# High and low halves for the first attention's projections, and a lead on unnormed halves for the last gated stage

## The chip, the cores and the metric

The kernel runs on one core of one Trainium2 chip, in one launch. The metric is the device time of that core in microseconds (us); lower is better. A core has five engines that run their own instruction streams side by side and meet at semaphores: TensorE (PE, the matrix products), VectorE (DVE), ScalarE (ACT), GpSimd (POOL) and SyncE (SP, which here issues the loads of the weights). Three runs of the kernel before gave 1784.17, 1782.44 and 3429.42 us, with a median of 1784.17 us.

## The reference

The program is a small network on 256 tokens of 1024 numbers. A first block has two layers: sliding window attention with 16 query heads, 4 key and value heads and a learned sink per head, then a feed forward stage (`ffn0`); and a gated delta rule mixer with its feed forward stage (`ffn1`). A second block has `ffn2`, a convolution mixer, `ffn3`, `ffn4`, a pooling and attention mixer (`pm_in`, `pm_out`) and `ffn5`. Ahead of each stage its input is normed. In the second block the norm's gain and shift come from a condition vector, and the stage's output is gated. The two places that matter here:

```python
u = rms_norm(h, mixer_norm[0])
qkv = u @ w_in                      # q 1024, k 256, v 256 columns
q = partial_rope(rms_norm(q, q_gain), cos, sin)
k = partial_rope(rms_norm(k, k_gain), cos, sin)
...                                 # scores in a window, softmax with a sink, values
h = h + out.reshape(B, S, 1024) @ w_out

x = x + mod[:, 1, 2][:, None, :] * y          # y from the pooling and attention mixer
h = modulate(rms_norm_2(x, ffn_norm[1, 1]), mod[:, 2, 0], mod[:, 2, 1])
x = x + 0.5 * mod[:, 2, 2][:, None, :] * swiglu(h, ...)      # ffn5
```

All data are float32.

## The kernel before

**Layout.** The stream of activations `h` lies as 8 chunks of 128 features by 256 tokens. Every weight matrix is cut into units of 128 x 1024 numbers (512 KB). SP loads the units in one fixed order into a ring of five slots (`weight_ring`). A slot is free again when the unit's products are done (`unit_done`), or, for a unit that is split into halves, when its low half is written (`lo_ready`).

**Two kinds of product.** A plain product (L1074, L1259, L2355) multiplies float32 weights out of the ring by float32 activations; the trace shows it as two weight loads and two matmul records. A split product has the weights and the activations each as a high half, rounded to the type `float32r`, and a low half, the rest, and adds three products of that type: high by high, high by low, low by high (`split_product_whole`, L657 to L659). For a unit of weights ACT writes the high half (`split_hi`, L611) and DVE the low half (`split_lo`, L618) into slots of `w_hi` and `w_lo`. A slot can be written when the unit that used it before is done.

**First attention.** `attn_in` has 12 units: 10 tiles of keys and queries and 2 of values. `attn_pe` goes through turns t = 0 to 10. A turn has the product of tile t (L1074), a sum of squares over the heads of tile t-1 (L1055) and the rotation of tile t-2 (L1062); the scores of a group of four heads follow behind turns 5, 7 and 10. ACT (`attn_act`) copies and squares tile t (L1111, L1112) and takes root t-1 (L1121, L1123). DVE (`attn_dve`) norms tile t (L1149) and rotates tile t-1 (L1156 to L1159); from turn 4 on it also masks scores (L1306), takes maxima (L1316 to L1327) or divides the probabilities (L1334 to L1342). Each engine does its list in the written order. Behind the tiles come, for each of four groups b, transposes of the probabilities (L1212), the values (L1228 to L1230), a copy of the result into `mix` (`mix_copy_act`, L1291) and the output product (`out_product_pe`, L1259), two units and eight chunks n. The last group hands its chunks to `residual_dve`, where DVE adds them to `h` (L540), with the squares for the next norm beside it (L334 on ACT, L418 on DVE).

**The norm.** `norm_pe` sums the squares with a product by ones (L406), ACT takes logarithm and exponential (L357, L359), and DVE and ACT write the normed halves (`norm_dve`, L447 and L473 or L475; `norm_halves_act`, L379 or L381). PE runs a few products with no use (`warm_pe`, L395) meanwhile.

**Stages with a lead.** Where a norm's number k is in `RAW` (3, 4, 6, 7, 8), the stage's first four units (`SPLIT`) don't wait for the norm: ACT and DVE write halves of h times gain (`lead_hi_act` L282, `lead_lo_dve` L293), `lead_pe` multiplies those (L315 to L317), and the result is scaled by the root afterwards (`lead_scale_dve`, L847 and L849). Norm 9, ahead of `ffn5`, is not in `RAW`: there, three units wait for the normed halves chunk by chunk (`ffn_up_pe`, L650, L653). Ahead of it is the output product of the last mixer, `pm_out`, whose units and values are split already (L1252 to L1254, `mix_low_dve` L1300). In `ffn_dve` and `ffn_act` a unit's split stands at a fixed place of the list: units 4 and 5 of a gated stage around the sum of the first pair.

Of the kernel before, what the change touches and what calls it, by code (L numbers as in the profile page):

```python
# [15 lines left out]
F32 = mybir.dt.float32  # L16
# [8 lines left out]
T = 256  # L25
# [93 lines left out]
def build(nc, dram, out_dram):  # L119
    with ExitStack() as ctx:  # L120
# [140 lines left out]
        RAW = (3, 4, 6, 7, 8)  # L261
        GAIN_WITH_ROOT = (0, 1, 9) + RAW
        AFTER = {3: 1, 4: 2, 6: 3, 7: 4, 8: "pm_in"}
# [40 lines left out]
        def lead_pe(pe, k):  # L304
# [4 lines left out]
            for j in range(SPLIT):  # L309
                s = split_wait(pe, AFTER[k], j)  # L310
                pe.wait_ge(h_ready, C * (k - 1) + lead_bank_read(k, j))
                for c in range(C):
                    if j == 0:
                        pe.wait_ge(lead_lo_ready, leads_until(k, c))
                    nc.tensor.matmul(ps[:, j, 0:n], w_hi[:, s, c], lead[:, c, 0, 0:n], start=c == 0, stop=False, skip_group_check=True)  # L315
                    nc.tensor.matmul(ps[:, j, 0:n], w_hi[:, s, c], lead[:, c, 1, 0:n], start=False, stop=False, skip_group_check=True)
                    last = nc.tensor.matmul(ps[:, j, 0:n], w_lo[:, s, c], lead[:, c, 0, 0:n], start=False, stop=c == C - 1, skip_group_check=True)  # L317
                    if j == 0 and c == SUM_BEHIND[k]:
# [100 lines left out]

        def norm_gain_dve(dve, k):  # L420
# [18 lines left out]
        def norm_dve(dve, k):  # L439
# [4 lines left out]
            for c in range(C):  # L444
# [16 lines left out]
                if k in (3, 6) and c == 2:  # L461
                    split_lo(dve, AFTER[k], SPLIT - 1)
# [17 lines left out]
        HALVES_OF = {1: 0, 2: 1, 3: 2, 4: 3, 6: 4, 7: 5, 8: 6, 9: 7}  # L480

        def u_count(k, c):
            return U_BASE[k] + c + 1

# [83 lines left out]
        SPLIT_RUNS = [(("ffn0",), SPLIT), (("gdn_gates", "gdn_in", "gdn_out"), GDN_SPLIT), (("ffn1", "ffn2"), SPLIT), (("ffn3", "ffn4", "pm_in", "pm_out", "ffn5"), SPLIT)]  # L568
# [4 lines left out]
        for names, slots in SPLIT_RUNS:  # L573
            units = [FIRST_UNIT[name] + j for name in names for j in range(dict(UNITS)[name])]
# [50 lines left out]
        def norm_split_act(act, k, q):  # L625
# [363 lines left out]
        ax = Carver(gdn_tiles, GX)  # L989
        sco = [[ax.cut(4, 384) for _ in range(4)]]  # L990
# [7 lines left out]
        sco.append([at_.cut(4, 384) for _ in range(2)])  # L998
        assert at_.at == end

        stats = [[at_.cut(4, 3)] + [at_.cut(4, 2) for _ in range(7)] for _ in range(4)]
        alibi = at_.cut(8, 384)
# [101 lines left out]

        def attn_act(act):
            for t in range(11):
# [24 lines left out]
            mix_copy_act(act, 0, 0)  # L1131
            turned_copy_act(act, 0, 1)
# [108 lines left out]
        def out_product_pe(pe, which, b, n):  # L1241

            k = (0, 8)[which]
            first = FIRST_UNIT[LIN[k]] + 2 * b
# [3 lines left out]
            for kk in range(2 if which == 1 else 0):  # L1248
                s = split_wait(pe, "pm_out", 2 * b + kk) if n == 0 else PM_OUT_SLOTS[2 * b + kk]
                hi, lo = w_slot(s)  # L1250
# [4 lines left out]
                if n == C - 1:  # L1255
                    last.then_inc(unit_done, 1)
            for kk in range(2 if which == 0 else 0):
                s = take_unit(pe, first, kk) if n == 0 else (first + kk) % RING
                last = nc.tensor.matmul(ps[:, bank, at:at + T], ring[:, s, n], mix[:, 2 * b + kk], start=(b == 0 and kk == 0 and n < 4),  # L1259
                                        stop=(b == 3 and kk == 1), skip_group_check=True)  # L1260
# [26 lines left out]
        def mix_copy_act(act, which, b):  # L1287
            act.wait_ge(pv_ready, 4 * which + b + 1)
            oc = head_of(which, b, 0)[4]
            if which == 0:  # L1290
                nc.scalar.activation(mix[:, oc:oc + 2].rearrange("p a b -> p (a b)"), ps[:, 4, :], ACT.Copy).then_inc(mix_ready, 1)  # L1291
            else:
                nc.scalar.activation(mix_halves[:, oc:oc + 2].rearrange("p a b -> p (a b)"), ps[:, 4, :], ACT.Copy).then_inc(mix_hi_ready, 1)

        def mix_low_dve(dve, b):

            oc = head_of(1, b, 0)[4]
            flat = lambda x: x.rearrange("p a b -> p (a b)")
            dve.wait_ge(mix_hi_ready, b + 2)
# [1276 lines left out]
        def moba_pe(pe):  # L2576
# [40 lines left out]
            norm_pe(pe, 9)  # L2617
# [62 lines left out]
        def moba_dve(dve, steps):  # L2680
# [41 lines left out]
            dve.wait_ge(mix_hi_ready, 1)  # L2722
# [10 lines left out]
            mix_low_dve(dve, 0)  # L2733
# [3 lines left out]
            mix_low_dve(dve, 1)  # L2737
# [31 lines left out]
        def act_program(act):  # L2769
# [32 lines left out]
            split_hi(act, 5, SPLIT - 1)  # L2802
            ffn_act(act, 5)

        def dve_program(dve):
# [4 lines left out]
            norm_first_dve(dve)  # L2810
            angles_dve(dve, steps)
# [270 lines left out]
```

## Time and profile before

| what | value |
|---|---|
| median of three runs | 1784.17 us |
| the profiled execution | 1785.92 us, span 1784.1 us |
| TensorE busy | 1743.2 us (98%) |
| VectorE busy | 1402.2 us (79%) |
| ScalarE busy | 1028.9 us (58%) |
| GpSimd busy | 85.3 us (5%) |
| granted TensorE clock, mean | 0.998 |
| moved by DMA | 374.07 MB |

The span runs from the first to the last instruction of one profiled execution; that execution's own time is 1.8 us longer. Busy is the time in which an engine had an instruction in it. Matmuls overlap in the engine, so a long busy time doesn't mean that the engine is at its peak, and the distance between two starts says more than the length of a record. A granted clock of 1.00 is 2.4 GHz, one of 0.50 is 1.2 GHz.

### The profile page before, as it was taken

The numbers are of one execution on the slowest core, as the hardware profiler recorded it, in microseconds if no ns is written. First come the engines' busy times: TensorE is split into PE (matmuls) and PEld (weight loads), VectorE is DVE, ScalarE is ACT, GpSimd is POOL, SyncE is SP. The second block draws the span as 40 slices with busy tenths as digits, with TensorE's granted clock in tenths as the row PEclk, the third lists the DMA queues.
The fourth block names the chain that finished last, engine by engine and source line by source line (L and its number), as shares of the span: only waits on it lengthen the run. The fifth ranks groups of instructions, "written<-read, shape, count | busy, mean of one in ns | idle before, by whom it ended". The sixth has DMA issues, their size and how long they took to land.

```text
span 1784.1 us, 34769 instructions
## 1 busy us (share of the span) xinstructions
PE 1743.2 (98%) x14142; PEld 1557.7 (87%) x14142; DVE 1402.2 (79%) x2369; ACT 1028.9 (58%) x1744; POOL 85.3 (5%) x163
## 2 busy tenths in 40 slices
PE   7999999989999999999999999999999999999998
PEld 6888888888888898889988888888898889988887
DVE  4758879777766488889988977898989898867664
ACT  3657765657866477654655422665556555566553
POOL 0000001000000000001001100000101010000000
PEclk9999999999999999999999999999999999999999
DMA  5255559343332355568788933788878887436552
GB/s 196 91 186 200 190 190 347 133 144 131 102 116 96 106 199 205 189 232 308 281 294 286 337 132 112 270 307 282 321 254 311 281 318 268 161 131 205 189 189 95
DMA packets 102829, 374.07 MB, mean 210 GB/s; under 512 B 11440, under 2 KB 11600, under 8 KB 102544
## 3 DMA queue, kind: packets, MB, share of 16 engines
q1 hardware_dynamic: 80352, 289.77, 46.3%
q0 software_dynamic: 22320, 82.09, 13.4%
q8 instruction: 112, 1.84, 0.4%
q14 instruction: 45, 0.37, 0.1%
HBM read 370.74 MB, written 1.08 MB: 208 GB/s over the span
## 4 chain that ended last, share of the span: by engine, by line
PE 86%; DVE 6%; ACT 3%; issue 2%; DMA 1%; DVEq 0%; SPq 0%; ACTq 0%
PE ps L650 37%; PE ps L653 20%; PE ps L657 3%; PE ps L658 3%; PE ps L659 3%; PE ps L1074 2%; PE ps L748 2%; DVE weights_lo L618 2%; PE ps L1259 1%; PE ps L2355 1%; ACT weights_hi L611 1%; DVE arena L2474 1%; PE ps L2381 1%; DMA ffn_tiles<-in_ada 1%; PE ps L1440 1%
## 5 line engine op out<-in xcount | busy, mean ns | idle before, releaser
L618 DVE TENSOR_TENSOR weights_lo<-weight_ring,weights_hi 128x1024 fp32r<-128x1024 f32 x493 | 601.7, 1222 | 136.1 <-ACT weights_hi L611 135.4
L611 ACT ACTIVATE weights_hi<-weight_ring 128x1024 fp32r<-128x1024 f32 x493 | 518.0, 1057 | 161.9 <-PE ps L650 106.5
L650 PE MATMUL ps<-u_halves,weights_hi 128*128 128x512 f32 x2048 | 495.0, 391 | 0.9 <-DVE u_halves L473 0.5
L650 PEld LDWEIGHTS ps<-u_halves,weights_hi 128*128 128x128 f32 x2048 | 376.3, 188 | 75.8 <-DVE weights_lo L618 1.0
L653 PEld LDWEIGHTS ps<-u_halves,weights_lo 128*128 128x128 f32 x2048 | 266.0, 191 | 10.5 <-DVE weights_lo L618 0.3
L653 PE MATMUL ps<-u_halves,weights_lo 128*128 128x256 f32 x2048 | 274.2, 283 | 0.2
L650 PE MATMUL ps<-act_halves,weights_hi 128*128 128x512 f32 x952 | 231.6, 391 | 1.0 <-DVE weights_lo L618 1.0
L650 PEld LDWEIGHTS ps<-act_halves,weights_hi 128*128 128x128 f32 x952 | 173.4, 188 | 33.8 <-DVE weights_lo L618 1.4
L887 DVE SCALAR_TENSOR_TENSOR ffn_tiles<-ffn_tiles,cond 128x1024 f32<-128x1024 f32 x144 | 175.3, 1219 | 4.8 <-DMA ffn_tiles<-in_ada 4.6
L780 ACT ACTIVATE ffn_tiles<-ps 128x512 f32<-128x512 f32 x128 | 76.0, 594 | 144.1 <-PE ps L653 143.8
L653 PEld LDWEIGHTS ps<-act_halves,weights_lo 128*128 128x128 f32 x1088 | 142.3, 191 | 6.4
L653 PE MATMUL ps<-act_halves,weights_lo 128*128 128x256 f32 x1088 | 145.8, 282 | 0.0
L657 PE MATMUL ps<-u_halves,weights_hi 128*128 128x256 f32 x456 | 136.8, 300 | 4.7 <-DVE u L2062 2.9
L858 DVE TENSOR_TENSOR ffn_tiles<-ps,ffn_tiles 128x512 f32<-128x512 f32 x128 | 88.3, 689 | 59.3 <-ACT ffn_tiles L780 59.2
L983 POOL DMA_DIRECT2D ffn_tiles<-in_ada x144 | 76.1, 529 | 1215.8 <-DVE ffn_tiles L887 785.9
L658 PE MATMUL ps<-u_halves,weights_hi 128*128 128x256 f32 x456 | 129.5, 284 | 0.0
L659 PE MATMUL ps<-u_halves,weights_lo 128*128 128x256 f32 x456 | 129.3, 284 | 0.0
L334 ACT ACTIVATE u<-h 128x256 f32<-128x256 f32 x88 | 35.8, 414 | 118.4 <-DVE h L913 74.9
L657 PEld LDWEIGHTS ps<-u_halves,weights_hi 128*128 128x128 f32 x456 | 87.6, 192 | 9.2 <-DVE u L2062 3.3
L658 PEld LDWEIGHTS ps<-u_halves,weights_hi 128*128 128x128 f32 x456 | 87.9, 193 | 1.1 <-issue 1.0
L659 PEld LDWEIGHTS ps<-u_halves,weights_lo 128*128 128x128 f32 x456 | 87.8, 193 | 0.0
L793 ACT ACTIVATE ffn_tiles<-ffn_tiles 128x256 f32<-128x256 f32 x130 | 53.6, 413 | 35.5 <-DVE ffn_tiles L858 17.1
(350 smaller groups left out, 2374.6 us busy)
## 6 DMA issues: line engine op xcount, KB each, us to landing
weight_ring<-in_w SPq DMA_DIRECT2D x545, 512.0 KB, 4.0
ffn_tiles<-in_ada POOLq DMA_DIRECT2D x144, 512.0 KB, 5.8
scaled<-gates_scratch POOLq DMA_DIRECT2D x8, 512.0 KB, 5.5
arena<-in_alibi POOLq DMA_DIRECT2D x1, 1536.0 KB, 6.6
h<-in_x SPq DMA_DIRECT2D x4, 256.0 KB, 3.8
out<-u SPq DMA_DIRECT2D x4, 256.0 KB, 2.4
consts<-in_consts SPq DMA_DIRECT2D x1, 592.0 KB, 10.0
cond<-in_cond SPq DMA_DIRECT2D x1, 512.0 KB, 10.7
```

What stands on the lines that cost most here:

```text
L611: nc.scalar.activation(w_slot(s)[0], ring[:, n % RING], ACT.Copy).then_inc(hi_ready, 1)
L618: nc.vector.tensor_tensor(lo, ring[:, n % RING], hi.bitcast(F32), ALU.subtract).then_inc(lo_ready, 1)
L650: return nc.tensor.matmul(ps[:, bank], hi, halves, start=start, stop=stop, skip_group_check=True)
L653: return nc.tensor.matmul(ps[:, bank, 0:T], lo, halves[:, 0], start=start, stop=stop, skip_group_check=True)
L657: nc.tensor.matmul(out, hi, halves[:, 0], start=start, stop=False)
L658: nc.tensor.matmul(out, hi, halves[:, 1], start=False, stop=False)
L659: return nc.tensor.matmul(out, lo, halves[:, 0], start=False, stop=stop)
L780: nc.scalar.activation(corr[:, f % 2], ps[:, b:b + 2, T:2 * T], ACT.Copy).then_inc(corr_ready, 1)
L793: nc.scalar.activation(sgb[:, f % 2], src, ACT.Silu, bias=bias).then_inc(sg_ready, 1)
L858: nc.vector.tensor_tensor(gu[:, f % 3], ps[:, b:b + 2, 0:T], corr[:, f % 2], ALU.add).then_inc(gu_ready, 1)
L887: nc.vector.scalar_tensor_tensor(ada_ring[:, r], ada_ring[:, r], 1.0, cond[:], ALU.mult, ALU.mult, accum_out=mods[:, n:n + 1]).then_inc(ad ...
L983: pool.dma_start(ada_ring[:, n % 3], dram["ada"][n]).then_inc(ada_loaded[n % 3], 16)
```

## The change

Seven of the ten key and query tiles (t = 3 to 9) and the eight output units of the first attention become split products. For that `first_halves_act` and `first_halves_dve` write halves of the normed input (8 operations each), `split_hi` and `split_lo` get 15 units more, one at the end of each of the turns 0 to 9 and five behind them, and `mix_low_dve` writes the low half of each group's values on DVE. The score tiles of group 0 move from the room of `w_hi` to another place of the arena, since `w_hi` is in use now. Norm 9 joins `RAW`. `lin_residual_dve` replaces `residual_dve` ahead of it: behind each residual stands the low half of the chunk before, then seven additions of squares in pairs, where the sum on PE had three terms before. The sum stands behind chunk 3 of the lead's second unit. ACT writes the high halves of `ffn5`'s units 2 and 3 behind the last chunk. The `warm_pe` products of norm 9 are gone with its `norm_pe` at the end of `moba_pe`.

```diff
+PLAIN_QK = 3
+COUNT = dict(UNITS, attn_q=10 - PLAIN_QK)
-        RAW = (3, 4, 6, 7, 8)
-        GAIN_WITH_ROOT = (0, 1, 9) + RAW
+        RAW = (3, 4, 6, 7, 8, 9)
+        GAIN_WITH_ROOT = (0, 1) + RAW
-        SUM_BEHIND = {3: 5, 4: 4, 6: 4, 7: 4, 8: 4}
+        SUM_BEHIND = {1: (1, 7), 3: (0, 5), 4: (0, 4), 6: (0, 4), 7: (0, 4), 8: (0, 4), 9: (1, 3)}
+        def add_pairs_dve(dve, k):
+            for n, (to, other, after) in enumerate(((1, 0, 0), (3, 2, 0), (5, 4, 0), (3, 1, 2), (7, 6, 0), (5, 3, 4), (7, 5, 6))):
+                if after:
+                    dve.wait_ge(sq_added, adds_until(k, after))
+                else:
+                    dve.wait_ge(sq_ready, 8 * k + to + 1)
+                nc.vector.tensor_tensor(u[:, to], u[:, to], u[:, other], ALU.add).then_inc(sq_added, 1)
+        def lin_residual_dve(dve, k, gated, next_ffn):
...
+            for c in range(C):
...
+                nc.vector.scalar_tensor_tensor(h[:, c], ps[:, bank, at:at + T], g, h[:, c], ALU.mult, ALU.add).then_inc(h_ready, 1)
+                if c:
+                    lead_lo_dve(dve, k + 1, c - 1)
+            lead_lo_dve(dve, k + 1, C - 1)
...
+            add_pairs_dve(dve, k + 1)
+            split_lo(dve, next_ffn, 2)
-        SPLIT_RUNS = [(("ffn0",), SPLIT), ...
+        SPLIT_RUNS = [(("attn_q", "attn_out", "ffn0"), SPLIT), ...
                 if k == 9:
-                    if c == 1:
+                    if c == C - 1:
                         split_hi(act, q, 2)
+                        split_hi(act, q, SPLIT - 1)
@@ attn_pe
+                if PLAIN_QK <= t < 10:
+                    s = split_wait(pe, "attn_q", t - PLAIN_QK)
+                    for k in range(C):
+                        if t == PLAIN_QK:
+                            pe.wait_ge(u_lo_ready, 8 * HALVES_OF[0] + k + 1)
+                        last = split_product_whole(ps[:, 4 + t % 2, 0:T], w_hi[:, s, k], w_lo[:, s, k], u_halves[:, k], k == 0, k == C - 1)
+                    last.then_inc(unit_done, 1)
+        def first_halves_act(act):
+            for c in range(C):
+                act.wait_ge(u_ready, u_count(0, c))
+                nc.scalar.activation(u_halves[:, c, 0], u[:, c], ACT.Copy).then_inc(u_hi_ready, 1)
+        def first_halves_dve(dve):
+            for c in range(C):
+                dve.wait_ge(u_hi_ready, 8 * HALVES_OF[0] + c + 1)
+                nc.vector.tensor_tensor(u_halves[:, c, 1], u[:, c], u_halves[:, c, 0].bitcast(F32), ALU.subtract).then_inc(u_lo_ready, 1)
+        def attn_split(turn):
+            q = turn - (10 - PLAIN_QK)
+            return ("attn_q", turn) if q < 0 else ("attn_out", q)
@@ attn_act, end of a turn
+                if t < 10:
+                    split_hi(act, *attn_split(t))
@@ attn_dve, end of a turn, and behind the turns
+                if t < 10:
+                    split_lo(dve, *attn_split(t))
             probs_dve(dve, steps, 0, 1)
             mask_scores_dve(dve, steps, 0, 3)
             maxima_dve(dve, steps, 0, 2)
+            mix_low_dve(dve, 0, 0)
             maxima_dve(dve, steps, 0, 3)
+            split_lo(dve, "attn_out", 3)
             probs_dve(dve, steps, 0, 2)
+            mix_low_dve(dve, 0, 1)
             probs_dve(dve, steps, 0, 3)
+            split_lo(dve, "attn_out", 4)
+            split_lo(dve, "attn_out", 5)
+            mix_low_dve(dve, 0, 2)
+            split_lo(dve, "attn_out", 6)
+            split_lo(dve, "attn_out", 7)
+            mix_low_dve(dve, 0, 3)
@@ out_product_pe: the three split products for both mixers, the plain one removed
-                last = nc.tensor.matmul(ps[:, bank, at:at + T], ring[:, s, n], mix[:, 2 * b + kk], start=(b == 0 and kk == 0 and n < 4),
...
@@ dve_program
             norm_first_dve(dve)
+            first_halves_dve(dve)
             angles_dve(dve, steps)
...
-            residual_dve(dve, 8, True, "lin", 5)
+            lin_residual_dve(dve, 8, True, 5)
             norm_dve(dve, 9)
-            split_lo(dve, 5, SPLIT - 1)
```

## Rows read from the trace of the kernel before

**Rows 1.** Busy time by stretch of the first attention: stretch, its length, busy per engine.
```profile
25.00:68.00 43.00, 42.79 (x245) 36.73 (x244) 26.64 (x70) 19.54 (x68) 0.00 (x0) 1.00 0.32 110
```

**Rows 2.** Timeline of PE, plain products, transposes, norm: start, length, instruction.
```profile
26.07 3.62 PE L1074 MATMUL ps<-u,weight_ring 128*128 128x256 f32 x16
...
70.16 1.47 PE L1212 MATMUL ps<-consts,gdn_tiles 128*128 128x128 f32 x12
...
76.45 3.62 PE L1259 MATMUL ps<-mix,weight_ring 128*128 128x256 f32 x16
...
102.03 10.63 PE L1259 MATMUL ps<-mix,weight_ring 128*128 128x256 f32 x48
113.59 1.53 PE L406 MATMUL ps<-u,consts 128*128 128x256 f32 x6 [0.94 <-ACT u L334]
```

**Rows 3.** Timeline of PE, first and last of 24 split products in a row.
```profile
1514.82 0.28 PE L657 MATMUL ps<-u_halves,weights_hi 128*128 128x256 f32 x1
...
1517.57 0.28 PE L659 MATMUL ps<-u_halves,weights_lo 128*128 128x256 f32 x1
```

**Rows 4.** Timeline of DVE in the first attention.
```profile
24.99 0.48 DVE L1149 SCALAR_TENSOR_TENSOR arena<-arena,cols 128x256 f32<-128x256 f32 x1 [6.92 <-ACT arena L1123]
...
39.86 0.48 DVE L1149 SCALAR_TENSOR_TENSOR arena<-arena,cols 128x256 f32<-128x256 f32 x1 [2.70 <-ACT arena L1123]
...
41.39 1.94 DVE L1306 SCALAR_TENSOR_TENSOR gdn_tiles<-ps,consts 128x384 f32<-128x384 f32 x4
...
62.28 0.16 DVE L1334 TENSOR_TENSOR arena<-arena 128x8 f32<-128x8 f32 x1
...
64.29 0.35 DVE L1342 TENSOR_SCALAR gdn_tiles<-gdn_tiles,arena 128x256 f32<-128x256 f32 x1
...
75.15 1.74 DVE L1316 TENSOR_REDUCE arena<-gdn_tiles 128x12 f32<-128x1536 f32 x1
...
77.67 1.75 DVE L1316 TENSOR_REDUCE arena<-gdn_tiles 128x12 f32<-128x1536 f32 x1
```

**Rows 5.** Timeline of DVE: a low half of values; two low halves of weights.
```profile
1578.57 0.69 DVE L1300 TENSOR_TENSOR mix_halves<-ps,mix_halves 128x512 fp32r<-128x512 f32 x1 [3.85 <-ACT mix_halves L1293]
1579.52 2.36 DVE L618 TENSOR_TENSOR weights_lo<-weight_ring,weights_hi 128x1024 fp32r<-128x1024 f32 x2 [0.26 <-ACT weights_hi L611]
```

**Rows 6.** Timeline ahead of ffn0: unit 0's high half on ACT, first residual on DVE.
```profile
104.04 1.06 ACT L611 ACTIVATE weights_hi<-weight_ring 128x1024 fp32r<-128x1024 f32 x1
...
106.65 0.42 DVE L540 SCALAR_TENSOR_TENSOR h<-ps,h 128x256 f32<-128x256 f32 x1 [0.29 <-PE ps L1259]
```

**Rows 7.** Timeline around norm 9, all engines: residuals, squares, sum, fifth unit's end.
```profile
1581.80 1.65 DVE L540 SCALAR_TENSOR_TENSOR h<-ps,half_gate,h 128x256 f32<-128x256 f32 x4
...
1585.15 0.42 DVE L418 TENSOR_TENSOR u<-u 128x256 f32<-128x256 f32 x1
1585.48 0.48 DVE L540 SCALAR_TENSOR_TENSOR h<-ps,half_gate,h 128x256 f32<-128x256 f32 x1
...
1587.16 1.53 PE L406 MATMUL ps<-u,consts 128*128 128x256 f32 x6 [1.73 <-ACT u L334]
...
1603.68 3.82 PE L650 MATMUL ps<-u_halves,weights_hi 128*128 128x512 f32 x16
```

**Rows 8.** Timeline around norm 6, a stage with a lead: high half, sum, norm, unit 5's low half.
```profile
1129.26 0.49 ACT L282 ACTIVATE lead_in_arena<-h,gain 128x256 fp32r<-128x256 f32 x1
...
1133.41 0.67 PE L406 MATMUL ps<-u,consts 128*128 128x256 f32 x2 [0.29 <-DVE u L418]
...
1135.33 0.87 DVE L447 SCALAR_TENSOR_TENSOR scaled<-h,gain,rstd 128x256 f32<-128x256 f32 x2
...
1145.87 1.21 DVE L618 TENSOR_TENSOR weights_lo<-weight_ring,weights_hi 128x1024 fp32r<-128x1024 f32 x1
```

**Rows 9.** Busy time by stretch, where the granted clock fell: the column ahead of the last two.
```profile
337.60:341.00 3.40, 1.28 (x11) 1.08 (x10) 2.77 (x5) 2.65 (x6) 1.85 (x4) 1.00 0.34 112
341.00:344.40 3.40, 3.40 (x17) 3.40 (x18) 3.33 (x5) 1.21 (x2) 0.22 (x1) 0.50 0.73 214
```

More of the change, by code:

```diff
@@ L460, in norm_dve @@
                     split_lo(dve, AFTER[k], SPLIT)
-                if k in (3, 6) and c == 2:
+                if k in RAW and k in (1, 3, 6, 9) and c == 2:
                     split_lo(dve, AFTER[k], SPLIT - 1)
@@ L566, in build @@
         assert ADA_BASE[6] == MOD_TILES
-        SPLIT_RUNS = [(("ffn0",), SPLIT), (("gdn_gates", "gdn_in", "gdn_out"), GDN_SPLIT), (("ffn1", "ffn2"), SPLIT), (("ffn3", "ffn4", "pm_in", "pm_out", "ffn5"), SPLIT)]
+        SPLIT_RUNS = [(("attn_q", "attn_out", "ffn0"), SPLIT), (("gdn_gates", "gdn_in", "gdn_out"), GDN_SPLIT), (("ffn1", "ffn2"), SPLIT), (("ffn3", "ffn4", "pm_in", "pm_out", "ffn5"), SPLIT)]
         PM_OUT_SLOTS = [0, 1, 4, 5, 2, 3, 4, 5]
@@ L573, in build @@
         for names, slots in SPLIT_RUNS:
-            units = [FIRST_UNIT[name] + j for name in names for j in range(dict(UNITS)[name])]
+            units = [FIRST_UNIT[name] + j for name in names for j in range(COUNT[name])]
             for at, n in enumerate(units):
@@ L988, in build @@
         vtok = at_.cut(2, 512)
-        ax = Carver(gdn_tiles, GX)
-        sco = [[ax.cut(4, 384) for _ in range(4)]]
         prT = at_.cut(12, P)
@@ L997, in build @@
         at_.at, end = reuse_at, at_.at
-        sco.append([at_.cut(4, 384) for _ in range(2)])
+        sco = [None, [at_.cut(4, 384) for _ in range(2)]]
         assert at_.at == end
         stats = [[at_.cut(4, 3)] + [at_.cut(4, 2) for _ in range(7)] for _ in range(4)]
+        alibi_at = at_.at
+        sco[0] = [at_.cut(4, 384) for _ in range(4)]
+        at_.at = alibi_at
         alibi = at_.cut(8, 384)
@@ L1131, in attn_act @@
             mix_copy_act(act, 0, 0)
+            split_hi(act, "attn_out", 3)
             turned_copy_act(act, 0, 1)
@@ L1247, in out_product_pe @@
                 pe.wait_ge(h_ready, 8 * k + n - 3)
-            for kk in range(2 if which == 1 else 0):
-                s = split_wait(pe, "pm_out", 2 * b + kk) if n == 0 else PM_OUT_SLOTS[2 * b + kk]
-                hi, lo = w_slot(s)
+            for kk in range(2):
+                if n == 0:
+                    split_wait(pe, LIN[k], 2 * b + kk)
+                hi, lo = w_slot(SPLIT_SLOT[split_at(LIN[k], 2 * b + kk)])
                 begin, end, acc = b == 0 and kk == 0 and n < 4, b == 3 and kk == 1, ps[:, bank, at:at + T]
@@ L1254, in out_product_pe @@
                 last = nc.tensor.matmul(acc, lo[:, n], mix_half(0, 2 * b + kk), start=False, stop=end, skip_group_check=True)
[L1255 to L1258, printed above, removed]
-                last = nc.tensor.matmul(ps[:, bank, at:at + T], ring[:, s, n], mix[:, 2 * b + kk], start=(b == 0 and kk == 0 and n < 4),
-                                        stop=(b == 3 and kk == 1), skip_group_check=True)
                 if n == C - 1:
@@ L1289, in mix_copy_act, with mix_low_dve @@
             oc = head_of(which, b, 0)[4]
[L1290 to L1297, printed above, removed]
+            nc.scalar.activation(mix_halves[:, oc:oc + 2].rearrange("p a b -> p (a b)"), ps[:, 4, :], ACT.Copy).then_inc(mix_hi_ready, 1)
+        def mix_low_dve(dve, which, b):
+            oc = head_of(which, b, 0)[4]
             flat = lambda x: x.rearrange("p a b -> p (a b)")
-            dve.wait_ge(mix_hi_ready, b + 2)
+            dve.wait_ge(mix_hi_ready, 5 * which + b + 1)
             nc.vector.tensor_tensor(flat(mix_halves[:, C + oc:C + oc + 2]), ps[:, 4, :], flat(mix_halves[:, oc:oc + 2].bitcast(F32)), ALU.subtract).then_inc(mix_ready, 1)
@@ L2732, in moba_dve @@
             split_lo(dve, "pm_out", 5)
-            mix_low_dve(dve, 0)
+            mix_low_dve(dve, 1, 0)
             probs_dve(dve, steps, 1, 1)
@@ L2736, in moba_dve @@
             split_lo(dve, "pm_out", 7)
-            mix_low_dve(dve, 1)
+            mix_low_dve(dve, 1, 1)
             split_lo(dve, 5, 0)
```

29 lines of the change are left out of this document (21 added, 8 removed).

## The prediction

> **What bounds the kernel now.** I read the chain of waits first: nearly all of it lies on TensorE. The table by stretch says the same of the first attention: from 25 to 68 us PE is busy 42.79 of 43.00 us, DVE only 26.64, ACT 19.54 [rows 1]. So cheaper products look like a gain, and spare DVE and ACT time looks like the place for the splits. But an average share doesn't say whether an engine with an ordered list is free when it is needed, so I then read the timelines of PE, DVE and ACT around both edits, and the stage ahead of `ffn3`, which already starts with a lead as `ffn5` shall.
>
> **Products.** A plain product is two records. In the row of 48 the start-to-start distance is (10.63 - 0.28) / 48 = 0.2156 us, the 0.28 being a single record's length [rows 2, 3], so a product costs 0.431 us and a unit of eight 3.45 us. The 24 records start 2.75 us apart from first to last, 0.1196 us each [rows 3]; three make a split product of 0.359 us, a unit of 2.87 us. The edit makes 7 x 8 + 8 x 8 = 120 products 0.072 us cheaper: 8.6 us on PE at most, 4.0 in the tiles and 4.6 in the output. The Trainium skill (TensorE: Matmul & The Clock Gate, Back-to-back issue gap) puts 256 columns at 2.4 GHz at N/2.4 + 2.5 = 109 ns; by that a split product would be 0.327 us and the 120 would save 12.5 us. The rows, with their alternating weight loads, say 120 ns, and I use them.
>
> **Tiles: the saving is eaten by DVE.** Start: DVE writes the low half of tile 3 only behind norming tile 0, so it is ready at 24.99 + 0.40 + 1.21 = 26.6 (start-to-start of the norming 0.40, estimated from its 0.48 as for the residuals below; low half 1.21) [rows 4, 8]. PE began tile 3 at 26.07 [rows 2]: +0.65 with the wake-up. The eight low halves of the input ahead of the angles delay only the angles, whose sine is behind ACT's table load anyway. If that cover is gone, it costs up to 8 x 0.33 = 2.6 us, which I keep for the range.
> A turn's base on DVE is 1.53 us (39.86 to 41.39, norming and rotation) [rows 4]. A second low half starts 2.36 - 1.22 = 1.14 us behind the first [rows 5, 8]. Masks take 1.9, maxima 77.67 - 75.15 = 2.5, probabilities 62.28 to 64.64 = 2.3 (8 pairs of scalings and their two small operations) [rows 4]. Turns 4 to 9 have 6 x (1.53 + 1.14) = 16.0, three masks 5.7, two maxima 5.0, one probabilities 2.3, and 1.1 for the last rotation: 30.2 us. Turn 4 starts on DVE at 39.86 + 0.65 - 3 x 0.58 = 38.8. I add 1.1 us of waits (turn 5's root is 2.87 + 0.86 + 1.7 = 5.4 us behind turn 4's, DVE has 4.5 of work there; a little in turn 7; the 0.86 is two of the small products, the 1.7 the scores, both estimates from the record distance) [rows 2]. That ends the last rotation at 70.1. PE's transposes began at 70.16 [rows 2]. So of PE's 4.0 us nothing arrives: small idle pieces ahead of tiles 3, 7, 8, 9 and about 1.9 us ahead of the transposes. Behind each low half in DVE's list the next norming waits, and PE's rotation and scores wait for that; this is in the sum.
> ACT gets 1.06 us per turn [rows 6] against 19.54 of 43 busy; only in turns 7 to 9, with the exponentials, is it full, and there the units are for the output, used 15 us later. Cost nothing; if ACT is late there, it is in the range. Ring and SP: a slot is now free at the low half instead of behind the product; loads start no later. The moved score tiles change no work.
>
> **First group of output.** Before, PE began it at 76.45 [rows 2]. Now it waits for `mix_low_dve`, which stands on DVE behind the third maxima; those end at 77.67, and nothing ahead of them moves (same start of transposes, same scores). 77.67 + 0.69 [rows 5] + 0.1 = 78.45: **+2.0 us**. Queued behind it on DVE are the fourth maxima and the probabilities of groups 2 and 3, which PE needs some 8 us or more later.
>
> **Output products.** 16 per group: 6.90 becomes 5.75, -1.15 per group. The last group began at 102.03 + 16 x 0.2156 = 105.48; now 105.48 + 2.0 - 3.45 = 104.0. There the chain changes: `ffn0`'s unit 0 uses the slot of output unit 4, free only now, and its halves stand ahead of the first residual on DVE: 104.0 + 0.2 + 1.06 + 1.21 = 106.5, as early as before (106.65) [rows 6]. From there DVE has 8 residuals of 0.39 and 5 additions of 0.33 (distances (1.65 - 0.48) / 3, and 1585.15 to 1585.48) [rows 7] without waiting for PE: 4.8 us, sum at 111.4 instead of 113.59 [rows 2]. **First attention: -2.1 us.** Bounds: -8.6 (all of PE's) and +3 (halves of the input uncovered, the 2.0 kept, half a unit regained).
>
> **Norm 9.** Removed: 1.73 us of idle, two of three sum products, five warm-up products, the slow start. By PE alone: output ends at 1585.4, four lead units 11.5, sum 0.4, unit 4 2.8: unit 5 could start at 1600.2. Before it starts at 1603.68 + 8 x 0.23 = 1605.5 [rows 7]: the lower bound is -5.3.
> DVE's list: from 1581.80 [rows 7] 8 residuals and 8 lead lows, 16 x 0.39 = 6.3; idle 1.5 (0.7 until ACT has the first square, the shift and the first high half, the high half 0.49 [rows 8]; the last chunk's high half 0.4 late; 0.4 between); 7 additions 2.3. Sum at 1592.1. PE stands behind chunk 3 of unit 1 at about 1591.5 and waits some 0.6. In the stage ahead of `ffn3` the first normed chunk came 1135.33 - 1133.41 = 1.92 behind the sum, and unit 5's low half was done 1147.08 - 1135.33 = 11.75 later, with everything that stands here too: 16 chunk operations, low halves 3 and 4, half gates, lead scaling [rows 8]. 1592.1 + 1.92 + 11.75 = 1605.8: **+0.3 us**. PE does units 1 to 4 earlier and then waits. Upper bound +2, if ACT's table load or unit 6 comes late too. The stage stays as it was from there.
>
> **Sum.** -2.1 + 0.3 = -1.8 us. Against the profiled execution's span of 1784.1 that is 1782.3 (its own time is 1.8 above its span); the median of the runs shown is at that span, so the predicted time is **1782.4 us**.
>
> **Rivals.**
> 1. *Partly hidden.* DVE and ACT overlap better than my lists, so half of each lower bound arrives: -4.3 - 2.6, **1777.3 us**. For it: DVE is idle 16 of 43 us now [rows 1]. Against: the idle time lies ahead of roots that PE delivers. Chance 0.19.
> 2. *PE sets the end everywhere.* -8.6 - 5.3: **1770.3 us**. Against: the first output group alone waits for a DVE operation that wasn't there. 0.03.
> 3. *Slower: the clock falls.* From 337.6 to 341.0 PE was busy 1.28 of 3.40 us, with a wait for DVE, and the next 3.4 us were granted 0.50, 1.2 GHz [rows 9]: 1.7 us of work lost. The new waits of 1.9 us ahead of the transposes and 2.0 us ahead of the first output product are like that one. It decides if both stretches get as empty as that; both falls cost 3.4, and -1.8 + 3.4 gives **1785.8 us**. Against: their neighbourhood is full of products. The Trainium skill (TensorE: Matmul & The Clock Gate, Part 1) says that throttled is the default and activity releases it; the rows agree. 0.15.
> 4. *Slower by the lists.* The input's low halves and turns 7 to 9 on ACT uncovered, +2 to +4: **1786.0 us**. 0.08.
> 5. *No effect.* Weight loads keep split products at the old pace: **1784.2 us**. The distance of the split products speaks against it [rows 3]. 0.03.
> My forecast, 1780.3 to 1784.4, has 0.52.
>
> **Range and chances.** 1778.5 to 1786.5 takes in the forecast, most of rivals 3 to 5 and the near part of rival 1. Two per cent, about what a measurement here tells from no change, is 36 us; no case reaches it: faster 0.01, same 0.98, slower 0.01.
>
> **What would show it.** In the changed trace: 0.36 us per split product; PE idle ahead of the transposes and of the first output product, released by DVE; that product near 78.4; the sum of norm 1 near 111.4; the sum of norm 9 about 5 us later relative to the last output product, and `ffn5`'s unit 5 released by its low half, some 20 us behind it. I am wrong if the transposes start well before 69 or after 72, if the clock is 0.50 in the first attention, or if unit 4 and 5 of `ffn5` follow without a wait.

## The result, and the profile after

The changed kernel took 1785.66 us (median of 11 executions, 1783.78 to 1791.81), the kernel before 1782.81 in the same session; the ratio is 1.0019, 95% interval 1.0010 to 1.0028. That is 2.9 us slower by the medians (1.8 to 5.0 by the interval), far inside 2%, where 1.8 us faster was forecast. One of the 11 executions of the kernel before took 3429.42 us; it isn't in the ratio. The profiled execution alone would have misled: its span is 1781.9 us against 1784.1 before. Both are single draws. The spans of 35 other executions of the kernel before run from 1777.9 to 1786.5 us, with a median of 1782.1, so the one of [rows 1 to 9] was a long one. The trace says where: from the sum of norm 2 to the sum of norm 3 (the gated delta mixer, which the change doesn't edit) it took 325.15 us, the trace of the changed kernel 322.47. Over all 13 traces of this document that distance runs from 320.2 to 325.2 us, in a stage that none of them edits.

I read the new trace by the distances between landmarks, not by the span. First the stretch of [rows 1] and the landmarks on PE in the first attention (start, length, instruction, idle before and who ended it):

```profile
25.00:68.00 43.00, 40.87 (x307) 36.36 (x308) 36.51 (x79) 28.58 (x79) 0.00 (x0) 1.00 0.34 111
```

```profile
26.11 0.70 PE L1097 MATMUL ps<-arena,consts 128*128 128x256 f32 x2 [0.21 <-DVE arena L1214]
27.30 0.36 PE L691 MATMUL ps<-u_halves,weights_hi 128*128 128x256 f32 x1 [0.48 <-ACT arena L1170]
...
71.04 1.53 PE L1288 MATMUL ps<-consts,arena 128*128 128x128 f32 x12 [1.57 <-DVE arena L1224]
...
79.36 0.38 PE L1328 MATMUL ps<-mix_halves,weights_hi 128*128 128x256 f32 x1 [1.80 <-DVE mix_halves L1367]
...
111.67 1.53 PE L411 MATMUL ps<-u,consts 128*128 128x256 f32 x6 [0.94 <-ACT u L339]
```

DVE went from 26.6 to 36.5 busy us of 43, and PE now waits for it: 1.57 us ahead of the transposes, 1.80 ahead of the first output product. The row of tile 3 names ACT for its wait of 0.48, but DVE's low half of that tile, in the first row below, ended later, at 27.20, 0.1 us ahead of the product. In the kernel before the small products of tile 0 (the row of 26.11) began at 25.53 and the sum of norm 1 at 113.59 [rows 2], 88.06 us apart; now it is 85.56, 2.50 less.

DVE: the low half of tile 3, then `mix_low_dve` behind the third maxima, then the low half of `ffn0`'s unit 0 and the first residuals:

```profile
25.98 1.22 DVE L651 TENSOR_TENSOR weights_lo<-weight_ring,weights_hi 128x1024 fp32r<-128x1024 f32 x1
...
76.09 1.74 DVE L1383 TENSOR_REDUCE arena<-arena 128x12 f32<-128x1536 f32 x1
...
78.62 0.68 DVE L1367 TENSOR_TENSOR mix_halves<-ps,mix_halves 128x512 fp32r<-128x512 f32 x1
79.22 1.74 DVE L1383 TENSOR_REDUCE arena<-arena 128x12 f32<-128x1536 f32 x1
...
105.90 1.23 DVE L651 TENSOR_TENSOR weights_lo<-weight_ring,weights_hi 128x1024 fp32r<-128x1024 f32 x1 [2.51 <-ACT weights_hi L644]
107.04 1.41 DVE L573 SCALAR_TENSOR_TENSOR h<-ps,h 128x256 f32<-128x256 f32 x4
```

Norm 9 and `ffn5`, the start of the residuals, the sum, and the first products of units 4 and 5 (compare [rows 7]), DVE and then PE:

```profile
1579.22 0.87 DVE L509 SCALAR_TENSOR_TENSOR h<-ps,half_gate,h 128x256 f32<-128x256 f32 x2
...
1587.16 2.56 DVE L432 TENSOR_TENSOR u<-u 128x256 f32<-128x256 f32 x7
```

```profile
1589.87 0.67 PE L411 MATMUL ps<-u,consts 128*128 128x256 f32 x2 [0.48 <-DVE u L432]
...
1599.06 1.32 PE L687 MATMUL ps<-u_halves,weights_lo 128*128 128x256 f32 x7 [0.78 <-DVE weights_lo L651]
...
1603.18 1.19 PE L684 MATMUL ps<-u_halves,weights_hi 128*128 128x512 f32 x4 [0.18 <-DVE weights_lo L651]
```

Unit 5 starts 23.96 us behind the first residual; before it was 1605.5 - 1581.8 = 23.7. So +0.3 there, as forecast, and the first attention gains. (Between outer landmarks, from the sum of norm 8 to the sum behind `ffn5`, the nine traces with norm 9's part have 271.4 us and the four without it 271.0, so +0.4.) What loses stands between the two edits, at the end of `ffn0`, in a stage in which no product and no list was edited. PE after:

```profile
315.65 1.12 PE L687 MATMUL ps<-act_halves,weights_lo 128*128 128x256 f32 x8
319.66 0.67 PE L411 MATMUL ps<-u,consts 128*128 128x256 f32 x2 [2.89 <-DVE u L423]
```

and before:

```profile
317.57 1.12 PE L653 MATMUL ps<-act_halves,weights_lo 128*128 128x256 f32 x8
318.71 0.67 PE L406 MATMUL ps<-u,consts 128*128 128x256 f32 x2
```

The last product of `ffn0` is 1.92 us earlier, and the sum of norm 2 behind it 0.95 us later. DVE there, after:

```profile
308.64 0.42 DVE L947 SCALAR_TENSOR_TENSOR h<-ps,h 128x256 f32<-128x256 f32 x1
312.21 1.23 DVE L651 TENSOR_TENSOR weights_lo<-weight_ring,weights_hi 128x1024 fp32r<-128x1024 f32 x1 [3.14 <-ACT weights_hi L644]
...
315.09 1.23 DVE L651 TENSOR_TENSOR weights_lo<-weight_ring,weights_hi 128x1024 fp32r<-128x1024 f32 x1 [0.51 <-ACT weights_hi L644]
317.95 1.23 DVE L651 TENSOR_TENSOR weights_lo<-weight_ring,weights_hi 128x1024 fp32r<-128x1024 f32 x1 [1.64 <-ACT weights_hi L644]
319.10 0.42 DVE L423 TENSOR_TENSOR u<-u 128x256 f32<-128x256 f32 x1
```

and before:

```profile
311.25 1.23 DVE L618 TENSOR_TENSOR weights_lo<-weight_ring,weights_hi 128x1024 fp32r<-128x1024 f32 x1 [0.27 <-ACT weights_hi L611]
...
317.00 1.23 DVE L618 TENSOR_TENSOR weights_lo<-weight_ring,weights_hi 128x1024 fp32r<-128x1024 f32 x1 [1.65 <-ACT weights_hi L611]
```

ACT after, the high half that the third of these waits for:

```profile
316.87 1.06 ACT L644 ACTIVATE weights_hi<-weight_ring 128x1024 fp32r<-128x1024 f32 x1 [1.81 <-PE ps L687]
```

These are the first three units of the gated delta net, split ahead of time. Slots are dealt out in turn (`at % slots`) over a run of stages. The change put 15 units ahead of `ffn0` in its run `("attn_q", "attn_out", "ffn0")`, and 15 is not a multiple of four. So the delta net's units inherit the slots of `ffn0`'s units 69, 70 and 71 where they had 68, 69 and 70, and the third high half waits for the very last product of `ffn0`. Relative to the end of `ffn0`'s products everything in DVE's list comes one unit (2.88 us) later: the third low half began 1.7 us ahead of that end (317.00 against 318.7) and now begins 1.2 us behind it (317.95 against 316.8). The last square additions stand behind that low half, and PE's sum waits for them.

### The profile page after: what moved, and what is told of

It is laid out like the page before. It is cut to its first block, busy times and chain, and to the rows that moved or that the text cites. A ratio compares the mean times of both kernels' runs of the same rounds, so it can differ in the third digit from the quotient of the medians.

```text
span 1781.9 us, 35131 instructions
## 1 busy us (share of the span) xinstructions
PE 1735.7 (97%) x14280; PEld 1555.7 (87%) x14280; DVE 1427.7 (80%) x2409; ACT 1047.6 (59%) x1774; POOL 85.7 (5%) x163
## 4 chain that ended last, share of the span: by engine, by line
PE 86%; DVE 7%; ACT 3%; issue 2%; DMA 1%; DVEq 0%; SPq 0%; ACTq 0%
PE ps L684 38%; PE ps L687 21%; PE ps L691 3%; PE ps L692 3%; PE ps L693 3%; PE ps L782 2%; DVE weights_lo L651 2%; PE ps L2422 1%; ACT weights_hi L644 1%; DVE arena L2541 1%; PE ps L2448 1%; PE ps L1507 1%; PE ps L1627 1%; PE ps L1328 1%; PE ps L1508 1%
## 5 line engine op out<-in xcount | busy, mean ns | idle before, releaser
L651 DVE TENSOR_TENSOR weights_lo<-weight_ring,weights_hi 128x1024 fp32r<-128x1024 f32 x508 | 619.9, 1222 | 124.6 <-ACT weights_hi L644 124.0
L644 ACT ACTIVATE weights_hi<-weight_ring 128x1024 fp32r<-128x1024 f32 x508 | 533.0, 1057 | 152.8 <-PE ps L684 99.4
L684 PE MATMUL ps<-u_halves,weights_hi 128*128 128x512 f32 x2016 | 484.7, 391 | 0.7 <-DVE weights_lo L651 0.4
L684 PEld LDWEIGHTS ps<-u_halves,weights_hi 128*128 128x128 f32 x2016 | 370.3, 188 | 74.1 <-DVE weights_lo L651 1.6
L687 PEld LDWEIGHTS ps<-u_halves,weights_lo 128*128 128x128 f32 x2016 | 260.5, 191 | 12.1 <-DVE weights_lo L651 1.3
L687 PE MATMUL ps<-u_halves,weights_lo 128*128 128x256 f32 x2016 | 267.1, 283 | 1.4 <-DVE weights_lo L651 0.8
L691 PE MATMUL ps<-u_halves,weights_hi 128*128 128x256 f32 x512 | 153.2, 299 | 6.7 <-DVE u L2129 2.9
L692 PE MATMUL ps<-u_halves,weights_hi 128*128 128x256 f32 x512 | 145.4, 284 | 0.0
L693 PE MATMUL ps<-u_halves,weights_lo 128*128 128x256 f32 x512 | 145.1, 283 | 0.0
L691 PEld LDWEIGHTS ps<-u_halves,weights_hi 128*128 128x128 f32 x512 | 98.3, 192 | 12.8 <-issue 4.7
L692 PEld LDWEIGHTS ps<-u_halves,weights_hi 128*128 128x128 f32 x512 | 98.5, 192 | 1.2 <-issue 1.0
L693 PEld LDWEIGHTS ps<-u_halves,weights_lo 128*128 128x128 f32 x512 | 98.6, 193 | 0.0
```

What stands on the lines that cost most here:

```text
L644: nc.scalar.activation(w_slot(s)[0], ring[:, n % RING], ACT.Copy).then_inc(hi_ready, 1)
L651: nc.vector.tensor_tensor(lo, ring[:, n % RING], hi.bitcast(F32), ALU.subtract).then_inc(lo_ready, 1)
L684: return nc.tensor.matmul(ps[:, bank], hi, halves, start=start, stop=stop, skip_group_check=True)
L687: return nc.tensor.matmul(ps[:, bank, 0:T], lo, halves[:, 0], start=start, stop=stop, skip_group_check=True)
L691: nc.tensor.matmul(out, hi, halves[:, 0], start=start, stop=False)
L692: nc.tensor.matmul(out, hi, halves[:, 1], start=False, stop=False)
```

## The experiments

Theory S: these slots give back what the first attention gains. Theory A: the clock falls in PE's new waits in the first attention. First the parts of the change by themselves, and the waits filled. Times are medians, each beside the kernel before on the same chip.

**Repeat, and parts.** `e1_same` is the changed kernel. `e2_attn_only` has norm 9 as before, `e3_ffn5_only` has only norm 9's part:

```diff
# e2_attn_only                      # e3_ffn5_only: the other way round
-RAW = (3, 4, 6, 7, 8, 9)
+RAW = (3, 4, 6, 7, 8)
...
-            lin_residual_dve(dve, 8, True, 5)
+            residual_dve(dve, 8, True, "lin", 5)
...
```

> The changed kernel once more, unaltered, for a second trace and for the spread of the granted clock over its executions. Theory A (the clock): the two new waits of TensorE in the first attention, 1.6 us ahead of the transposes and 1.8 us ahead of the first output product, leave stretches emptier than any in the kernel before, and in a part of the executions the next stretch is granted 0.50, each time at a cost of 1.7 us or more; then times spread over 1782 to 1791 us and fall together with the mean clock (0.998 to 0.995), while the kernel before stays at 0.998 or 0.997. Theory B (the lead of ffn5): the same, but from the waits inside the lead. Theory C (chance): the difference of 2.9 us shrinks to under 1 us here.

> Only the first attention's part of the change; norm 9 and ffn5 as before. Theory A: the waits of TensorE in the attention are all there, so the time is that of the changed kernel within 1 us, some 2 to 4 us above the kernel before, with the clock at 0.996 to 0.997. Theory B: the schedule's gain of 2 us arrives, about 1781 us, with the clock at 0.998.

> Only norm 9's part of the change; the first attention as before. Theory A: within 1 us of the kernel before (the schedule gives +0.3 us; the stretch behind the last output product, which was the emptiest there, is fuller). Theory B: 3 to 5 us above the kernel before, with the clock at 0.996 to 0.997.

Measured against 1783.84 before: 1786.11 (ratio 1.0012, 1.0003 to 1.0021), 1785.42 (1.0010, 1.0001 to 1.0019) and 1783.72 (0.9998, 0.9990 to 1.0007). The repeat shows the loss again (0.5 to 3.7 us by the interval). The part of the first attention alone shows it too (0.2 to 3.4), and norm 9's alone is worth nothing that can be measured.

**Filled waits.** `e4_warm`:

```diff
+            pe.wait_ge(pjln_ready, 10)
+            warm_pe(6, 4)
             pe.wait_ge(rope_ready, 10)
             turn_probs_pe(pe, 0, 0)
...
+            pe.wait_ge(sc_read, 4)
+            warm_pe(3, 4)
             for b in range(4):
                 pe.wait_ge(mix_ready, b + 1)
-                if b == 0:
-                    pe.wait_ge(sc_read, 4)
```

> The changed kernel with four products of no use on TensorE (1.7 us) ahead of each of the two new waits in the first attention, behind everything they must not overwrite; they fit into the waits within 0.1 us. Theory A: the clock is back at 0.998 or 0.997, and the time is 1.5 to 2.5 us below the kernel before, 4 to 5 below the changed one. Theory B or C: no difference from the changed kernel beyond 1 us.

1786.00 us, ratio 1.0016 (1.0007 to 1.0026). In its trace PE has neither wait: eight extra records, 1.89 us, stand in each. Nothing was gained, so a clock that falls behind these two waits isn't the cause of the loss.

**The slots.** `e5_slots` (the changed kernel), and the same shift alone in the kernel before, `e6_before_shift`:

```diff
# e5_slots
-s = PM_OUT_SLOTS[out] if 0 <= out < C else at % slots
+s = PM_OUT_SLOTS[out] if 0 <= out < C else (at + (names[0] == "attn_q")) % slots
# e6_before_shift
-s = PM_OUT_SLOTS[out] if 0 <= out < C else at % slots
+s = PM_OUT_SLOTS[out] if 0 <= out < C else (at + 3 * (names[0] == "ffn0")) % slots
```

> The changed kernel, with only the slots of its first run of split units turned by one, so that ffn0 and the gated delta net's first three units get the slots that they had before the change. Theory S (the slots at the end of ffn0 give back what the first attention gains): TensorE's wait of 2.89 us ahead of the sum of norm 2 goes, DVE's wait for a high half there falls from 3.14 us to under 0.5, the sum of norm 2 starts some 2.9 us earlier (near 316.8), and the time is 2 to 3 us below the changed kernel's, 1 to 2 us below that of the kernel before. Theory A (the clock in the attention's own new waits): nothing changes there, within 0.5 us of the changed kernel, about 2 us above the kernel before.

> The kernel before, with only ffn0's slots turned by three, as the change turns them, and no other part of the change. Theory S: the same wait appears alone, DVE about 3.1 us for a high half and TensorE about 2.9 us ahead of the sum of norm 2; the time is 2.5 to 3 us above the kernel before. Theory A: no difference, within 0.5 us. Third theory (the last units of ffn0 wait because in the changed kernel TensorE comes there earlier, the slots have no part in it): no difference either.

Against 1783.24 before: 1782.76 (0.9996, 0.9985 to 1.0006) and 1787.31 (1.0020, 1.0012 to 1.0029). PE at the end of `ffn0` in the second, with none of the change's products in it:

```profile
316.83 1.12 PE L653 MATMUL ps<-act_halves,weights_lo 128*128 128x256 f32 x8
320.84 0.67 PE L406 MATMUL ps<-u,consts 128*128 128x256 f32 x2 [2.90 <-DVE u L418]
```

and in the first:

```profile
318.10 1.12 PE L687 MATMUL ps<-act_halves,weights_lo 128*128 128x256 f32 x8
319.24 0.67 PE L411 MATMUL ps<-u,consts 128*128 128x256 f32 x2
```

The wait comes with the shift and goes with it: theory S holds. The third theory, that PE merely comes early, falls: in `e6_before_shift` nothing ahead of it was faster. The size in time is less neat: e5 came out only 0.5 us below the kernel before instead of 1 to 2, e6 4.1 above instead of 2.5 to 3. Both intervals (-2.7 to +1.1 us, +2.1 to +5.2) still hold what was expected, so by themselves these times don't contradict the landmarks. From e1 to e5, each against the kernel before beside it, the time falls by 2.8 us.

**DVE's order.** `e7_order` is e5 with two moves in `attn_dve`, `e8_mixlow` with the second alone:

```diff
-                if t < 10:
+                if t < 8:
                     split_lo(dve, *attn_split(t))
             probs_dve(dve, steps, 0, 1)
+            split_lo(dve, "attn_out", 1)
+            split_lo(dve, "attn_out", 2)
             mask_scores_dve(dve, steps, 0, 3)
+            mix_low_dve(dve, 0, 0)
             maxima_dve(dve, steps, 0, 2)
-            mix_low_dve(dve, 0, 0)
```

> The kernel of e5_slots, and on DVE two moves in the first attention: the low halves of output units 1 and 2 stand behind the second group's probabilities instead of in turns 8 and 9, and the low half of the first mixed group stands ahead of the third maxima instead of behind them. If TensorE's waits ahead of the transposes and of the first output product are set by DVE's list, as the prediction has it, the first output product starts near 76 us instead of 79.4, and the time is 3 us below e5_slots (1.5 if the end of the first attention is by then set by the residuals on DVE and not by TensorE). If the saved time of the products is lost elsewhere (TensorE's pace, weight loads), no difference to e5_slots within 0.5 us.

> The kernel of e5_slots with the second of the two moves of e7_order alone: the low half of the first mixed group ahead of the third maxima. The prediction's +2.0 us for the first output group comes from that place in the list: the first output product starts about 2.3 us earlier, near 77, with TensorE's wait of 1.80 us ahead of it gone; what of it reaches the end is 1 to 2.3 us below e5_slots. If the sum of norm 1 is bound by DVE's additions and not by TensorE, 0.

1779.47 us (0.9983, 0.9974 to 0.9991) and 1780.72 (0.9989, 0.9978 to 1.0000). PE in e7:

```profile
25.86 0.70 PE L1097 MATMUL ps<-arena,consts 128*128 128x256 f32 x2 [0.21 <-DVE arena L1214]
...
69.42 1.53 PE L1290 MATMUL ps<-consts,arena 128*128 128x128 f32 x12 [0.44 <-DVE arena L1224]
...
76.42 0.39 PE L1330 MATMUL ps<-mix_halves,weights_hi 128*128 128x256 f32 x1 [0.48 <-DVE mix_halves L1369]
...
109.80 1.53 PE L411 MATMUL ps<-u,consts 128*128 128x256 f32 x6 [0.94 <-ACT u L339]
```

Against the changed kernel the first output product moved by 2.7 us (50.56 behind the first row, where it was 53.25), and 1.6 of it reached the end of the first attention (83.94 us between the outer rows against 85.56). 0.86 went into a new wait for DVE ahead of a later group's transposes, at 85.14; the last 0.2 I didn't trace. e7 beats both kernels: 3.8 us below the kernel before (1.6 to 4.6).

**What the split tiles bring.** `e9_out_only` is e7's order with plain tiles, `e10_order_attn` is e7 without norm 9's part, `e11_slots_warm` is e5 with e4's filled waits:

```diff
# e9_out_only
-PLAIN_QK = 3
+PLAIN_QK = 10
-            first_halves_act(act)
...
-                if t < 10:
-                    split_lo(dve, *attn_split(t))
+                if t == 7:
+                    split_lo(dve, "attn_out", 0)
...
-            first_halves_dve(dve)
...
# e10_order_attn
-RAW = (3, 4, 6, 7, 8, 9)
+RAW = (3, 4, 6, 7, 8)
...
```

> The kernel of e7_order with the ten query and key tiles plain again, as before the change: only the eight output units of the first attention are split (their slots come out as ffn0 had them before), and the low and high halves of the input are gone. If the tiles' split products bring PE almost nothing because DVE has the low halves to write (the prediction's 'the saving is eaten by DVE'), the transposes start near 70.2 as before the change instead of 69.4, the sum of norm 1 near 110.5, and the time is 0 to 0.7 us above e7_order. Rival: PE's 4.0 us from the tiles do arrive at the end of the first attention, then this kernel is 3 to 4 us above e7_order.

> The kernel of e7_order with norm 9 and the start of ffn5 as before the change. The prediction has this part at +0.3 us and the run of that part alone showed nothing: 0 to 0.4 us below e7_order. Rival: the part is worth its removed idle (up to 5.3 us on PE), then this kernel is 2 us or more above e7_order.

> The kernel of e5_slots with four products on idle data ahead of each of TensorE's two waits in the first attention (behind the last scores ahead of the transposes, and ahead of the first output product). The profile of e5_slots has two stretches at half clock there, and 4 of its 12 executions have a mean clock of 0.995 or 0.996. Theory A2 (those drops come from the two emptier stretches): the executions near 0.995 go, and the median falls by about 1 us below e5_slots. Rival (the drops come at the chip's own times, whatever the kernel does there): clock and time as e5_slots, within 0.5 us.

Against 1783.10 before: 1779.49 (0.9980, 0.9969 to 0.9991), 1780.02 (0.9985, 0.9972 to 0.9997), 1782.92 (0.9992, 0.9980 to 1.0005). By time e9, without the split tiles, is level with e7, as expected; by landmarks the tiles bring 1.66 us (the first attention takes 85.60 us in e9, 83.94 in e7), more than the 0.7 I had allowed. Part of that is e9's own: its transposes come 45.24 us behind tile 0's small products, 0.6 later than in the kernel before, where I had expected them as before. Norm 9's part is nothing that can be measured either way again. The filled waits did nothing for the time again and the mean clock is lower than e5's, so theory A2 falls too.

**The ledger.** A is the time from tile 0's small products to the sum of norm 1, B from there to the sum of norm 2, both worked out from the timelines; "time" is the median less that of the kernel before, "clock" the mean granted clock over the executions less that of the kernel before beside it.

| kernel | A, us | B, us | time, us | clock |
|---|---|---|---|---|
| before | 88.06 | 205.12 | | |
| e3, norm 9 alone | 88.06 | 205.10 | -0.1 | 0.0000 |
| e6, shift alone | 88.06 | 207.99 | +4.1 | -0.0010 |
| after (e1) | 85.56 | 207.99 (207.96) | +2.9 (+2.3) | (-0.0009) |
| e2, attention alone | 85.56 | 208.56 | +1.6 | -0.0012 |
| e4, filled | 85.52 | 208.18 | +2.2 | -0.0008 |
| e5, slots | 88.53, two falls | 205.08 | -0.5 | -0.0006 |
| e11, slots, filled | 87.05, one fall | 205.10 | -0.2 | -0.0013 |
| e8, mix_low | 86.23, one fall | 205.10 | -2.5 | -0.0005 |
| e10, order, no norm 9 | 85.40, one fall | 205.44 | -3.1 | -0.0002 |
| e7, order | 83.94 | 205.12 | -3.8 | +0.0001 |
| e9, output only | 85.60 | 205.12 | -3.6 | +0.0004 |

In ten of the 13 traces B is within 0.05 us of 205.12 or of 207.99: 2.87 us more with the shifted slots, and none without. e2, e4 and e10 have 0.2 to 0.6 us more on top, lost in the middle of `ffn0`, 157 us behind the sum of norm 1; e2's trace shows a wait of 0.27 there for a low half. A repeats as well, but for stretches at 1.2 GHz; one such fall costs 1.5 us there (85.40 against 83.94; 88.53 against 85.56 for two).

What is left between the landmarks' sum (for the changed kernel -2.50 + 2.87 + 0.26 = +0.6; falls in A left out) and the time goes roughly with the clock column: +2.2 for the changed kernel (+1.7 in its repeat e1), +1.8 for e5, +2.1 for e11, +1.2 for e6, 0.1 for e7, -1.4 for e9. It isn't strict: e2 has +0.6 at a clock of -0.0012, e10 +0.7 at -0.0002. Single executions say the same. The changed kernel's 22 average 1787.0 us at a mean clock of 0.996 (10 of them), 1785.8 at 0.997 (7) and 1784.2 at 0.998 (3). The 99 of the kernel before that stood beside the experiments average 1784.8 at 0.997 (21) and 1783.8 at 0.998 (59). So at equal clock the changed kernel is 0.4 to 1.0 us slower, about the +0.6 of the landmarks, and the rest of its 2.9 us comes with a lower mean clock. This is a correlation over few executions, not an experiment.

## Why the prediction was wrong

- **The number**: 1785.66 us lies inside the range of 1778.5 to 1786.5, and close to rival 3's 1785.8. Both are luck: the main forecast had the sign wrong, and rival 3 gets to its number by falls behind two waits that the runs rule out as the cause. Against the kernel before the forecast was -1.8 us and the result +2.9.
- **Products**: right. The first 24 records of tile 3 begin at 27.30 and the last at 30.12, 0.12 us apart.
- **Tiles eaten by DVE**: right for this order. Tile 3 waits 0.48, two later tiles wait 0.64 and 0.55, and the transposes come 44.93 us behind the first small products against 44.63 before, 0.3 later. I had the whole 4.0 us as lost. In e7, where two low halves left turns 8 and 9, the transposes come 43.56 us behind, 1.1 earlier than in the kernel before, so that much of it can be had.
- **First output group, +2.0**: right, 53.25 us behind the small products against 50.92, +2.3. In e8, with `mix_low_dve` moved, PE's wait of 1.80 is gone.
- **First attention, -2.1**: -2.50 by the landmarks, by the chain that I had: the first residual starts right behind the low half of `ffn0`'s unit 0 (105.90 to 107.13), and the sum 4.6 us later, where I had 4.8.
- **Norm 9, +0.3**: +0.3 to +0.4 by the landmarks, -0.1 (-1.8 to +1.3) by e3. The sum of norm 9 stands 5.3 us later than before behind the sum of norm 8; I had written about 5, counted from the last output product.
- **The failed step** is none of these terms but one that the sum doesn't have. The sum adds the two edits and so puts everything between them at nothing, without a reason; of the moved slots it has only that unit 0 of `ffn0` takes the slot of output unit 4. The edit to `SPLIT_RUNS` also turns the slots of all 72 units of `ffn0`, and at its other end, 200 us later, three low halves come one unit later on DVE, ahead of the additions that PE's sum needs: +2.87 us, shown with the shift alone (e6) and undone alone (e5). With it the sum is -2.1 + 0.3 + 2.9 = +1.1. That turns the sign but isn't yet the measured +2.9; what is missing is in the next point.
- **Rival 3, the clock**: a fall behind one of its two waits does occur, in one of the four traces that have the whole wait ahead of the first output product, unfilled (e5, at 81.8 us, below), but filling both waits left the time as it was (e4, e11). So they aren't the cause. But the changed kernel's executions have a lower mean clock than those before, and by the ledger that goes with the other 1 to 2 us. Falls occur behind other stretches, below. Which of them carries the mean isn't settled: only one execution of each kernel has a trace.
- **Rivals 1, 2, 4 and 5** didn't occur; e7 reaches, by two moves in a list, half of the lower bound for the first attention (-4.1 of -8.6).

## What to carry to other kernels

A counter that deals out buffers in turn links everything behind it: before adding units at its front, take the number modulo the slots, and look at who inherits the last slots and what stands behind that work in its engine's list. When a change is worth a few microseconds in 1800, compare distances between landmarks of the two traces, stage by stage. Here most repeat to 0.1 us, where spans of one kernel differ by 8.6 us; but look at each stage in several traces first, since one stage that nobody edits ranges over 5 us. And low halves on a list belong where the engine waits anyway, not at the end of every turn: of the 4.1 us that e7's first attention is shorter than before, 1.6 came from the order alone. e9, which splits only the output units, is as fast by time with much less added.

## What the runs showed of the hardware

The clock doesn't fall at the same stretch in each execution. In e1 a fall comes right behind the wait at the end of `ffn0`; in the changed kernel's own trace the same wait is not followed by one (stretch, its length, busy PE, PEld, DVE, ACT, POOL; clock, DMA):

```profile
315.60:319.00 3.40, 0.84 (x4) 0.80 (x5) 1.98 (x4) 1.44 (x3) 0.00 (x0) 0.98 0.57 183
319.00:322.40 3.40, 3.40 (x10) 2.64 (x9) 0.90 (x3) 1.67 (x5) 1.02 (x1) 0.52 0.35 125
```

```profile
316.00:319.40 3.40, 0.77 (x7) 0.56 (x5) 1.76 (x3) 1.06 (x1) 0.00 (x0) 1.00 0.44 159
319.40:322.80 3.40, 3.14 (x15) 2.81 (x16) 1.14 (x5) 1.86 (x5) 0.59 (x1) 1.00 0.48 154
```

Of the 5 traces with this wait 2 show a fall behind it (e1, e4), of the 8 without it none. The start of tile 3 is another such place. With split tiles the clock falls there in e5, e8, e10 and e11, 4 of 9 traces; with plain tiles in none of 4. Here e10, and e9 for comparison:

```profile
23.50:26.90 3.40, 1.84 (x8) 0.87 (x7) 1.62 (x2) 3.32 (x8) 0.00 (x0) 1.00 0.51 154
26.90:30.30 3.40, 3.40 (x18) 3.40 (x18) 2.72 (x5) 1.25 (x2) 0.00 (x0) 0.51 0.43 154
```

```profile
23.20:26.60 3.40, 2.33 (x10) 1.45 (x9) 0.48 (x1) 2.72 (x6) 0.00 (x0) 1.00 0.49 154
26.60:30.00 3.40, 3.40 (x18) 2.99 (x17) 1.58 (x4) 0.71 (x3) 0.00 (x0) 1.00 0.00 0
```

In the first PE was busy 1.84 us ahead of the fall, in the second 2.33 without one; but e7, with 1.88 us busy there, has none either. What goes with the fall is when the clock first rose. In the traces' clock records full clock begins at 13.3 to 13.6 us in all four with the fall, and at 13.2 to 13.6 in e9, e3 and the kernel before, which have plain tiles and no fall there (PE's first row of 32 records, near 12 us, takes 7.6 to 7.8 us in these seven). In the five traces with split tiles and no fall (the changed kernel's, e1, e2, e4 and e7) full clock begins at 11.7 to 12.6 or at 14.2 to 14.7 us (the row takes 7.1 to 7.2 or 8.1 to 8.2 us). So with about the same first rise four of four traces fall with split tiles, and none of three with plain ones.

The wait of 1.80 us ahead of the first output product has one fall behind it, in e5:

```profile
78.40:81.80 3.40, 1.61 (x14) 1.47 (x13) 3.26 (x8) 3.40 (x13) 0.00 (x0) 1.00 0.01 2
81.80:85.20 3.40, 3.40 (x18) 3.17 (x19) 3.19 (x13) 1.94 (x10) 0.00 (x0) 0.51 0.13 34
```

The fall of [rows 9], which my prediction read as a plain consequence of its stretch, is missing in e4, e8, e9 and e10. In e9 with the same 1.28 us of PE busy:

```profile
335.00:338.40 3.40, 1.28 (x12) 1.08 (x10) 2.66 (x5) 2.65 (x6) 0.98 (x2) 1.00 0.33 115
338.40:341.80 3.40, 3.40 (x27) 3.27 (x28) 3.33 (x5) 1.58 (x3) 1.09 (x2) 1.00 0.61 210
```

So a wait of 0.5 to 3 us on PE costs its own length, and behind it some traces show a fall that costs another 1.5 us. The Trainium skill (TensorE: Matmul & The Clock Gate, Part 1) says that the chip watches the activity in a window that runs freely and doesn't start with the kernel; that agrees with falls that come and go at one place between executions. That the falls at these places are what lowers the mean clock of the changed kernel is argued from 13 traces, not shown.
